# Six openings rearranged, and a slot given back three chunks later, in a fused four-layer kernel

## What is computed

```python
for layer in range(DEPTH):
    mod = (cond @ ada_w[layer] + ada_b[layer])[:, None, :]
    shift_m, scale_m, gate_m, shift_f, scale_f, gate_f = jnp.split(mod, 6, axis=-1)
    h = rmsnorm(x, norm_mix_g[layer]) * (1.0 + scale_m) + shift_m
    ...  # mixed = attention(h) or gated_deltanet(h): h @ w_in, heads, @ w_out
    x = x + gate_m * mixed
    h = rmsnorm(x, norm_ffn_g[layer]) * (1.0 + scale_f) + shift_f
    x = x + gate_f * swiglu(h, ffn_w_in[layer], ffn_w_out[layer])
```

## Time and profile before

| what | value |
|---|---|
| runs before, median (lowest to highest) | 3292.03 us (3288.44 to 3292.47) |
| the profiled execution's own time | 3289.55 us |
| its span | 3287.8 us |
| PE busy | 3101.1 us, 94% |
| DVE, ACT, POOL busy | 45%, 36%, 40% |
| mean granted clock of TensorE | 0.977 |

### The profile page before, as it was taken

The page is one execution under the profiler, slowest core; times in us unless marked ns, Lnnn a source line. Parts: engine busy times, 40 slices in busy tenths (PEclk is TensorE's granted clock), DMA queues, the critical chain, the costliest instruction groups (busy, mean ns, idle before and its releaser), DMA issues. The chain is left out here.

```text
span 3287.8 us, 39608 instructions
## 1 busy us (share of the span) xinstructions
PE 3101.1 (94%) x15656; PEld 2434.8 (74%) x15656; DVE 1465.4 (45%) x2350; ACT 1191.1 (36%) x1564; POOL 1305.0 (40%) x716
## 2 busy tenths in 40 slices
PE   5998999998999899999999999999999999999998
PEld 4864788876778778887873377888899783378886
DVE  5424331316775463545946426333356757321111
ACT  3255322223754432234235433223434335532222
POOL 2414444344452344443325543444301416544444
PEclk8999999998999899999999999999999999999999
DMA  8501243542100344442110013444454201122321
GB/s 312 218 13 39 103 178 140 199 143 77 69 26 1 115 158 169 166 166 96 61 62 1 27 64 128 173 166 177 150 174 172 90 26 46 50 81 81 116 86 61
DMA packets 56232, 360.16 MB, mean 110 GB/s; under 512 B 6032, under 2 KB 7184, under 8 KB 20880
## 3 DMA queue, kind: packets, MB, share of 16 engines
q1 hardware_dynamic: 54352, 348.63, 29.0%
q10 hardware_dynamic: 1728, 9.44, 0.7%
HBM read 355.95 MB, written 2.10 MB: 109 GB/s over the span
## 5 line engine op out<-in xcount | busy, mean ns | idle before, releaser
L403 POOL TENSOR_TENSOR W_LO<-ring,W_HI 128x2048 fp32r<-128x2048 f32 (+1 forms) x176 | 724.3, 4116 | 981.3 <-ACT W_HI L391 917.3
L466 PE MATMUL PS<-H_HI,W_HI 128*128 128x512 f32 (+1 forms) x1888 | 702.7, 372 | 24.6 <-POOL W_LO L403 11.0
L469 PE MATMUL PS<-H_LO,W_HI 128*128 128x512 f32 (+1 forms) x1888 | 699.9, 371 | 0.0
L470 PE MATMUL PS<-H_HI,W_LO 128*128 128x512 f32 (+1 forms) x1888 | 699.7, 371 | 0.0
L391 ACT ACTIVATE W_HI<-ring 128x2048 fp32r<-128x2048 f32 (+1 forms) x209 | 357.7, 1712 | 434.9 <-PE PS L456 413.1
L466 PEld LDWEIGHTS PS<-H_HI,W_HI 128*128 128x128 f32 x1888 | 357.4, 189 | 91.3 <-issue 30.4
L469 PEld LDWEIGHTS PS<-H_LO,W_HI 128*128 128x128 f32 x1888 | 357.7, 189 | 60.6 <-issue 0.2
L470 PEld LDWEIGHTS PS<-H_HI,W_LO 128*128 128x128 f32 x1888 | 357.5, 189 | 60.3
L454 PE MATMUL PS<-HID_HI,W_HI 128*128 128x512 f32 (+1 forms) x880 | 324.8, 369 | 7.2 <-DVE W_LO L403 4.0
L455 PE MATMUL PS<-HID_LO,W_HI 128*128 128x512 f32 (+1 forms) x880 | 323.7, 368 | 0.0
L456 PE MATMUL PS<-HID_HI,W_LO 128*128 128x512 f32 (+1 forms) x880 | 323.7, 368 | 0.0
(11 more groups left out here) (419 smaller groups left out, 5209.5 us busy)
## 6 DMA issues: line engine op xcount, KB each, us to landing
ring<-w_tiles SPq DMA_DIRECT2D x271, 1024.0 KB, 4.8
ring<-d_tiles SPq DMA_DIRECT2D x80, 704.0 KB, 4.1
WORK<-bias_tables ACTq DMA_DIRECT2D x4, 1792.0 KB, 10.0
X<-xT SPq DMA_DIRECT2D x1, 2048.0 KB, 18.6
outT<-H SPq DMA_DIRECT2D x8, 256.0 KB, 2.2
X<-ctxT SPq DMA_DIRECT2D x1, 1024.0 KB, 12.6
ACC<-rope_tables ACTq DMA_DIRECT2D x4, 256.0 KB, 6.3
CN<-consts SPq DMA_DIRECT2D x1, 707.0 KB, 8.8
```

The lines of the kernel that those rows point to most:

```text
L403: eng.tensor_tensor(W_LO[:, b, 0:w], ring[:, g % SLOTS, 0:w], W_HI[:, b, 0:w].bitcast(F32), ALU.subtract).then_inc(sig("tile_split"), 1)
L466: mm = pe.matmul(to, hi[:, cols(k, j)], x_hi(k), start=k == 0, stop=False)
L469: pe.matmul(to, hi[:, cols(k, j)], x_lo(k), start=False, stop=False)
L470: mm = pe.matmul(to, lo[:, cols(k, j)], x_hi(k), start=False, stop=k == n - 1)
```

## The change

- **Start.** The load of `X` is issued ahead of the fourth row tile of `ada0` in place of behind it.
- **Attention's opening.** ACT rounds the second tile in quarters between the chunks of `H_HI` (behind chunks 2, 4, 6 and 7), DVE makes its rest behind the last `H_LO`, ahead of its row tiles. ACT and GpSimd leave that tile out of their loops.
- **Up openings, all four.** DVE makes the second tile's rest ahead of the first gate's product, and does its first row tile behind that; GpSimd does neither.
- **Up stages with row tiles.** PE's wait for row tile m-1, and the count that gives its slot back, move from chunk 4 to chunk 7.
- **Convolution layer's opening.** The first tile is worked side by side, from `W_HI` buffer 0 and a new `GDN_LO` (no new memory: it lies over another region). ACT rounds it behind the last but one product of `down001` and the second tile's two halves behind the next square; DVE rests the first tile there and the second's first half behind the conditioning's end; GpSimd rests the other half when the norm is done. From the third tile on all is as before, a half later in the count.

```diff
@@ pe_up
-                    if side(name) and k == 4 and not (isinstance(m, int) and m == 0):
+                    if side(name) and k == DC - 1 and not (isinstance(m, int) and m == 0):
                         pe.wait_ge(sig("row_product"), products_until(layer + 1, half) + (m - 1) * per + per)
...
-                    if side(name) and k == 4 and j == 0 and not (isinstance(m, int) and m == 0):
+                    if side(name) and k == DC - 1 and j == 0 and not (isinstance(m, int) and m == 0):
                         mm.then_inc(tile_done, 1)
@@ dve_up
-                next_own(dve, name, rest_tile, m, u, i)
+                if opens(name) and isinstance(m, int) and m == 0:
+                    rest_second(dve, name)
+                else:
+                    next_own(dve, name, rest_tile, m, u, i)
...
             for m in range(UP):
-                dve_row_tile(dve, layer + 1, name, m + int(name[-1]) * (UP + 1), 2 * m + 1, 0)
+                if m or not opens(name):
+                    dve_row_tile(dve, layer + 1, name, m + int(name[-1]) * (UP + 1), 2 * m + 1, 0)
                 body(m, 2 * m, 0)
+                if m == 0 and opens(name):
+                    dve_row_tile(dve, layer + 1, name, int(name[-1]) * (UP + 1), 1, 0)
@@ pool_rest
                 if opens(name) and isinstance(m, int) and m == 0:
-                    rest_second(pool, name)
+                    return
@@ act_down
+                    if name == "down001" and m == DC - 1:
+                        round_first_gdn(act)
                     act_square(act, m - 1, c0, width)
+                    if name == "down001" and m == DC - 1:
+                        round_second_gdn(act)
@@ dve_down
+                if name == "down001" and m == DC - 1:
+                    rest_first_gdn(dve)
                 dve.wait_ge(tile_done, i * SLOTS + (g0 + u + 1))
...
+            if name == "down001":
+                rest_half(dve, 1, 0)
@@ rest_second
-        def rest_second(pool, name):
-            pool.wait_ge(sig("chunk_normed"), CHUNKS[name])
-            rest_tile(pool, name, 2 if side(name) else 1, 0, 1)
+        def rest_second(dve, name):
+            rest_tile(dve, name, 2 if side(name) else 1, 0, 1)
@@ dve_split_norm
+            if name == "attn_in":
+                rest_second(dve, name)
@@ gdn_in
+        def round_first_gdn(act):
+            g = G0["gdn_in"]
+            act.wait_ge(tile_loaded[g % SLOTS], (g // SLOTS + 1) * 16)
+            act.wait_ge(tile_done, G0["down001"] + DC - 1)
+            act.activation(W_HI[:, 0, :], ring[:, g % SLOTS, :], ACT.Copy).then_inc(sig("half_rounded"), 2)
+
+        def rest_first_gdn(dve):
+            dve.wait_ge(sig("half_rounded"), 2)
+            dve.tensor_tensor(GDN_LO[:, :], ring[:, G0["gdn_in"] % SLOTS, :], W_HI[:, 0, :].bitcast(F32),
+                              ALU.subtract).then_inc(sig("half_split"), 2)
@@ pe_gdn_in
+                if p == 0:
+                    pe.wait_ge(sig("half_split"), 2)
+                    pe_three_pair(pe, o, T, tile_cols, W_HI[:, 0, :], GDN_LO, lambda k: H_HI[:, k, :], lambda k: H_LO[:, k, :],
+                                  DC, normed).then_inc(tile_done, 1)
+                    continue
@@ pool_gdn_in
-                if p < 16:
+                if p == 0:
+                    pool.wait_ge(sig("chunk_normed"), 3 * DC)
+                elif p < 16:
                     rest_half(pool, p + 1, 0)
@@ block.sync
                 if name == "ada0":
-                    for t in range(SLOTS):
-                        load_one(t)
-                    sp.dma_start(X[:, :, 0:T], xT).then_inc(x_loaded, 16)
-                    for t in range(SLOTS, n):
+                    for t in range(n):
+                        if t == SLOTS - 1:
+                            sp.dma_start(X[:, :, 0:T], xT).then_inc(x_loaded, 16)
                         load_one(t)
@@ block.scalar
                 if layer < 2:
-                    if layer == 1:
-                        round_halves(act, 0, 0, 0)
                     act_split_norm(act, T, mod[:, 0:DC, 0], layer == 1, None if layer else
-                                   lambda k: round_first_piece(act, 2 + k // 2) if k in (0, 2) else None)
+                                   lambda k: round_first_piece(act, 2 + k // 2) if k in (0, 2) else None,
+                                   None if layer else "attn_in")
```

More of the change, by code:

```diff
@@ L161, in build_program @@
                 NORMED_CTX = side_norm.enter_context(nc.sbuf_tensor("NORMED_CTX", [P, DC, TC], F32))
+            with ExitStack() as first_rest:
+                GDN_LO = first_rest.enter_context(nc.sbuf_tensor("GDN_LO", [P, TILE], F32R))
             GATED = part("GATED", [P, 2, T], F32)
@@ L701, in dve_up @@
             if not side(name):
-                over_own(dve, name, body)
+                over_own(dve, name, body, apart_first=opens(name))
                 return
             for m in range(UP):
-                dve_row_tile(dve, layer + 1, name, m + int(name[-1]) * (UP + 1), 2 * m + 1, 0)
+                if m or not opens(name):
+                    dve_row_tile(dve, layer + 1, name, m + int(name[-1]) * (UP + 1), 2 * m + 1, 0)
                 body(m, 2 * m, 0)
+                if m == 0 and opens(name):
+                    dve_row_tile(dve, layer + 1, name, int(name[-1]) * (UP + 1), 1, 0)
         def pe_down(pe, layer, name, w):
@@ L977, in round_second @@
                 ins.then_inc(sig("tile_rounded"), 1)
-        def rest_second(pool, name):
-            pool.wait_ge(sig("chunk_normed"), CHUNKS[name])
-            rest_tile(pool, name, 2 if side(name) else 1, 0, 1)
-        CHUNKS = {"up000": 2 * DC, "up100": 4 * DC, "up200": 7 * DC, "up300": 11 * DC}
+        def rest_second(dve, name):
+            rest_tile(dve, name, 2 if side(name) else 1, 0, 1)
         def dve_split_norm(dve, name, gain, shift):
@@ L1143, in act_attn_in, with features @@
             g0 = G0["attn_in"]
-            def features(m, v, i):
-                next_own(act, "attn_in", round_tile, m, 2 * v, i)
-                act.wait_ge(tile_done, i * 4 + (g0 + 2 * v + 1))
+            def features(m, v, u, i):
+                if not isinstance(m, int) or m:
+                    next_own(act, "attn_in", round_tile, m, u, i)
+                act.wait_ge(tile_done, i * SLOTS + (g0 + u + 1))
                 act.activation(QK1[:, bass.ds(m * 2, 2), :],
@@ L1150, in features @@
                                ACT.Copy).then_inc(evac_done, 1)
-            over_pairs(act, 8, features, lambda m, v, i: None)
+            features(0, 0, 0, 0)
+            with act.Fori(0, 3) as i:
+                features(i * 2 + 1, 1, 2, i)
+                features(i * 2 + 2, 0, 4, i)
+            features(7, 1, 14, 0)
             for m in range(8, 12):
@@ L1179, in pool_attn_in @@
         def pool_attn_in(pool):
-            over_pairs(pool, 8, lambda m, v, i: next_own(pool, "attn_in", rest_tile, m, 2 * v, i), lambda m, v, i: None)
+            pool.wait_ge(sig("tile_split"), SPLIT["attn_in"] + 2)
+            with pool.Fori(0, 3) as i:
+                next_own(pool, "attn_in", rest_tile, i * 2 + 1, 2, i)
+                next_own(pool, "attn_in", rest_tile, i * 2 + 2, 4, i)
+            next_own(pool, "attn_in", rest_tile, 7, 14, 0)
             for m in range(8, 12):
@@ L2014, in build_program, with round_second_gdn @@
         CONVOLVED = [0, 1, 2, 3, 5, 6, 7, 8, 9, 10, 11, 12]
-        def round_halves(act, t, u, i):
-            g = G0["gdn_in"] + u
-            for j in range(2):
[L2020 to L2028, removed]
+        def round_first_gdn(act):
[7 more added lines that the diff above has]
+                              ALU.subtract).then_inc(sig("half_split"), 2)
+        def round_second_gdn(act):
+            g = G0["gdn_in"] + 1
+            act.wait_ge(tile_loaded[g % SLOTS], (g // SLOTS + 1) * 16)
+            for j in range(2):
                 act.activation(U_HI[:, j, :].rearrange("p (k c) -> p k c", k=DC), half_tile(g % SLOTS, j),
@@ L2035, in round_half @@
                 act.wait_ge(tile_loaded[g % SLOTS], (g // SLOTS + 1) * 16)
-                act.wait_ge(sig("half_done"), p)
+                act.wait_ge(sig("half_done"), p - 1)
             else:
@@ L2046, in rest_half @@
                                ALU.subtract).then_inc(sig("half_split"), 1)
-        def rest_halves(pool, t, u):
-            for j in range(2):
-                rest_half(pool, t, j)
         def half_tile(slot, j):
@@ L2112, in pe_gdn_in @@
                     continue
-                half(p, 0, o, normed if p == 0 else None).then_inc(sig("half_done"), 1)
+                half(p, 0, o).then_inc(sig("half_done"), 1)
                 if p == 5:
@@ L2149, in act_gdn_in @@
             for p in range(17):
-                if p < 16:
+                if 0 < p < 16:
                     round_half(act, p + 1, 0)
@@ L2224, in dve_gdn_in @@
             e0 = E0["gdn_in"]
```

(2 more changed lines are left out.)

## The result

The changed kernel takes 3353.37 us (median of 4 runs, 3352.52 to 3359.67) beside 3290.24 us for the kernel before on the same chip (4 runs, 3286.52 to 3292.47): a ratio of 1.0195, 95% interval 1.0184 to 1.0207. It is 1.95% slower; the forecast was 3350 us, with a range of 3318 to 3374.

The account below looks back on a forecast made before the run. TensorE, busy in 94% of the span, was taken to bound the kernel. 3289.55 - 13.0 - 6.7 + 0.4 + 62.4 + 2 + 15 = 3349.7, predicted as 3350 us, 1.8% slower; eight-in-ten range 3318 to 3374.

Parts of the forecast that it names:

- The release at chunk 7: Six up stages with side tiles: tiles come 2.07 us late, 24 waits of PE cost 62.4 us plus 15 of clock.
- Rival A: Up stages: the later release is absorbed if issue to rest's end becomes 12.0 us or less; total 3270 us; chance 0.06.
- Rival C: Up stages: the 24 waits cost only themselves, 50 us, without restart and clock; total 3320 us; chance 0.12.
- Rival B: Up stages: every one of 24 waits costs the clock, 38 us in place of 15; total 3373 us; chance 0.14.
- D: Openings give half, 9.7 us less, and attention's opening loses 3 us; total 3362 us; chance 0.08.
- E: Up stages: waits so few that the whole change nets out within 0.2%; chance 0.02.
- Second tile's rest on VectorE: Four up openings: PE's wait for the rest on GpSimd goes, gaining 13.0 us, or 12 if VectorE comes late.
- Convolution layer: Its opening: first tile's rounding and rest move under the last down products, gaining 6.7 us, bounds 5.1 to 8.3.
- Attention's opening: X starts the norm 1.4 us sooner, but ACT waits for the second tile's transfer: a loss of 0.4 us.
- Down tiles: First two down tiles, asked for by the same later releases: 0.3 us a stage, 2 us in all (0 to 6).

Follow-up runs that it names:

- experiment 2: The kernel before with PE's wait and release at chunk 7 instead of chunk 4, nothing else: 3370.29 us, ratio 1.0243.
- experiment 6: The changed kernel with attention's tiles issued ahead of constants, positions and context in SP's order: 3350.52 us, ratio 1.0184.
- experiment 1: The changed kernel with PE's wait and release back at chunk 4: 3280.24 us, ratio 0.9968.
- experiment 3: The changed kernel with PE's wait and release at chunk 6 instead of chunk 7: 3313.14 us, ratio 1.0071.
- experiment 4: The changed kernel with PE's wait and release at chunk 5 instead of chunk 7: 3279.65 us, ratio 0.9967.
- experiment 5: The changed kernel, but SP waits for VectorE's row product instead of PE's chunk 7 signal in the side up stages: 3275.90 us, ratio 0.9951.
- experiment 7: The kernel of experiment 1 with the second tile's rest in the four up openings back on GpSimd: 3285.02 us, ratio 0.9986.
- experiment 9: The changed kernel with the edits of experiment 5 and experiment 6, and the convolution layer's opening as before the change: 3275.75 us, ratio 0.9950.
- experiment 10: The changed kernel with the edits of experiment 5 and experiment 6, and X behind the fourth conditioning tile again: 3272.62 us, ratio 0.9939.

## Why the prediction was right, point by point

**The release at chunk 7, forecast 62.4 + 15 of clock, measured 77.4.** The mechanism is as forecast; that the sum agrees to 0.1 us is luck, since three differences cancel. Each step of the chain was met: issue 1.08 us before a gate (forecast 1.07), 13.85 us from issue to rest's end (14.03), 12.77 us behind the gate (12.96), 1.90 late (2.07), 11.43 us from there to the next gate (11.45), late and punctual products in turn, four late ones a stage, 24 in all. The price of one is 2.49 us (2.6 forecast), 59.8 in all. The other 17.6 us divide otherwise than forecast. 7 of the 24 waits were followed by half clock, two of them for twice as long as the others (forecast two in five); in the traces of experiments 2 and 6, with the same release, it was 8 and 9 of 24. And three transfers of product tiles took 7.96, 8.13 and 7.74 us where those at the same place in the other three stages took 6.6 to 6.7, which makes some 4 us and was not foreseen; 13.6 are left for the clock.

Experiments 1 and 2 show this term from both sides (76 us saved by undoing it alone, after paying 4.0 us of new waits; 78 lost by doing it alone), 3 and 4 give its slope and its edge, and 5 shows that it lies in SP's order. Rival A needed 12.0 us or less from issue to rest's end; it had 13.85. Rival C left out restart and clock, and both are there. Rival B, half clock after every wait, is refuted; so are D, whose openings give half and whose attention loses 3 us (12.0 and 6.5 us were gained, 0.2 lost), and E. The windows at 1.2 GHz behind two of the waits, and the one of the same place as in the earlier trace rows, which kept 2.4 GHz without its wait (us, busy of PE, PEld, DVE, ACT, POOL; granted clock; DMA share; GB/s):

```profile
386.50:389.50 3.00, 3.00 (x15) 2.47 (x14) 3.00 (x7) 0.23 (x1) 2.69 (x1) 1.00 0.00 0
597.60:604.40 6.80, 5.84 (x14) 4.64 (x15) 3.75 (x5) 1.91 (x1) 1.86 (x2) 0.50 0.45 189
1389.50:1392.90 3.40, 2.99 (x7) 2.42 (x8) 3.40 (x6) 0.00 (x0) 0.27 (x1) 0.50 0.76 301
```

The rule that was weighed against it, of the Trainium skill (TensorE: Matmul & The Clock Gate, section "HAM oscillation — how this bites in real kernels"), has the lower clock after each wait, and its waits are of about 3 to 5 us; here the lower clock came after 7 of 24: after all three long waits of 3.5 to 3.6 us, where the trace agrees, and after 4 of the 21 of 1.5 to 2.4 us.

**Second tile's rest on VectorE, forecast -13.0 (-12 if VectorE comes late), measured -12.0.** In the trace of after the second gate comes 11.18 to 11.20 us behind the first, not 10.89: the rest ends a little late, as the lower value supposed, 0.3 us in each of three. In `up300` it is 10.95. The reading of the 1.6 us in two of the openings as the clock's holds (experiment 7): that part isn't owed to the engine but to what the throttle did in that execution, so 8.7 of the 12.0 us are the edit's.

**Convolution layer, forecast -6.7 (5.1 to 8.3), measured -6.5 in the opening** (16.1 us from the rstd at 761.43 to where SP, released by the first tile, issues at 777.55, where it was 22.6 before; forecast 15.74) and 6.8 for the whole layer in experiment 9. From the timelines of ACT, DVE and GpSimd in the changed kernel:

```profile
751.43 1.92 ACT L2046 ACTIVATE W_HI<-ring 128x2048 fp32r<-128x2048 f32 x1 [6.35 <-DVE X L865]
...
761.43 0.63 ACT L921 ACTIVATE NORM_RSTD<-NORM_RSTD 128x512 f32<-128x512 f32 x1
...
777.61 1.03 ACT L2195 ACTIVATE WORK<-PS 128x1024 f32<-128x1024 f32 x1 [3.59 <-DVE WORK L2258]
```

```profile
753.46 2.29 DVE L2050 TENSOR_TENSOR GDN_LO<-ring,W_HI 128x2048 fp32r<-128x2048 f32 x1 [2.11 <-ACT W_HI L2046]
```

```profile
747.83 1.29 POOL L902 TENSOR_TENSOR NORM_SUM<-NORM_SUM,NORM_SQ 128x512 f32<-128x512 f32 x1
753.95 2.95 POOL L902 TENSOR_TENSOR NORM_SUM<-NORM_SUM,NORM_SQ 128x512 f32<-128x512 f32 x1 [4.83 <-ACT NORM_SQ L892]
```

The rounding and the rest lie under the last down products, as the step said.

**Attention's opening, forecast +0.4, measured +0.2** to the second evacuation (67.38 before, 67.60 after). X landed 2.5 us sooner (19.81, was 22.31), and VectorE began at 35.49 as worked out. ACT stood 5.61 us for the tile (landed 45.69) with chunk 3 of `H_HI` behind it; the last `H_LO` ended at 53.33, and VectorE's rest ran from 53.25 to 55.54. The forecast had 54.0 and 56.3, a little late because the tile itself came 0.6 us sooner. With the tile there (experiment 6) the second evacuation comes at 62.43, 5.0 us sooner than before, where the forecast had 4.4. X's move has 2.25 of that (experiment 10); the other 2.7 are the tile's and the rest's together, and no run has the tile early and the rest on GpSimd.

**Down tiles, forecast +2, measured +1.8** in the three places where nothing else lies between the stages. The forecast was for six stages, and in the other three this part can't be told from what follows.

**What was wrong in the working.** One remark: with chunk 4 as the limit, "5.4 us would have covered four (4.9) barely". They did not cover them: PE waited 1.7 us in two openings, 2.0 us lost in each (experiment 1). It was no term of the sum. And the base, one execution of the kernel before, had a favourable clock in layer 2's mixer: it took 2.8 us less there than the changed kernel and at least 1.6 us less than any of the ten experiments. That is as much as the sum falls short of the profiled execution (3349.7 beside 3352.52); the other differences cancel.

## What to carry to other kernels

A signal that gives back a buffer is a signal to the queue that refills it, and everything behind that refill in the queue's order moves with it: before moving one by three chunks, add up issue, transfer, rounding and rest, and compare the sum with the time until the next use; the slack here was 2.0 us and the move 4.1. If the consumer is to ask later, give the queue another release (the reader of that buffer, as in experiment 5), so that only the question is late. And a transfer brought forward is worth nothing while another one ends later: here the second tile, behind a megabyte and more of constants and context, had to be moved before the moves of X and of the rest, taken together, paid.

## What the runs showed of the hardware

**Loads beside an instruction fetch are sometimes longer.** In the side stages a row tile and a product tile are issued as a pair. The DMA view of one such pair in `up001` (583.7 to 591.9 us) and of the pair at the same place in `up201` (2235.9 to 2242.8), both in the changed kernel (packets, MB, share; then the load: KB and us to landing):

```profile
q1 hardware_dynamic: 288, 2.10, 68.1%
q8 instruction: 1, 0.02, 0.7%
issues: line engine op xcount, KB each, median us to landing
ring<-w_tiles SPq DMA_DIRECT2D x1, 1024.0 KB, 8.0
```

```profile
q1 hardware_dynamic: 288, 2.10, 80.5%
issues: line engine op xcount, KB each, median us to landing
ring<-w_tiles SPq DMA_DIRECT2D x1, 1024.0 KB, 6.7
```

The same bytes, 1.3 us more, and a packet of 0.02 MB of the instruction queue among them. From `up000` on there are 54 such second loads in the changed kernel (two loads issued within 1.3 us, and no third). In 44 no such packet falls between the pair's issue and the landing, and none of them took over 7.16 us (median 6.6); in 10 one does, and six of these took 7.7 to 8.2 us, four 6.65 to 6.9. Over this trace and those of experiments 2, 3 and 6 it is 178 without a packet, none over 7.25 us, and 38 with one, of which 21 took 7.7 to 8.4. The slack of 2.0 us at chunk 4 is longer than these 1.3 us; with chunk 7 they made a wait of 2.1 us one of 3.5. That the packet is the cause was not tried, the rows only go together.

**GpSimd stands while VectorE subtracts.** The norm's add on GpSimd takes 1.29 us alone and 2.95 beside VectorE's rest (the rows of L902 and L2050 above). It began at 753.95 and ended at 756.90, that is 1.15 us after the rest had ended at 755.75: about its own length. That is what the Trainium skill says (SBUF — State Buffer, section "SBUF: two separate sides": a VectorE operation with two inputs in SBUF and a GpSimd operation that reads SBUF want the same pair of ports, and whoever comes first holds it for the whole instruction), and the trace agrees with it.

**The clock falls after some of equal waits.** Of the 21 waits of some 2 us, 4 were followed by 1.2 GHz, 17 were not; in the traces of experiments 2 and 6 it was 5 of 21 and 7 of 22. All eight of these waits that were longer, 3.46 to 3.74 us in the three traces, had it. The openings of `up000` and `up200` lost 1.6 us that way before the change and nothing in experiment 7, with waits as long (2.4 us). What tells the short ones apart stays open.
